# Chunked delta rule and attention layer on one core: which waits the scan's operands have, the order of turns and sums, and when masks are made

## The reference

```
h = rms_norm(x, norm_w);  proj = h @ w_in            # q, k, v, z, beta, decay, sw_q, sw_k, sw_v, sw_z
qkv = silu(conv5(q, k, v));  q, k = l2_norm(q) * 128**-0.5, l2_norm(k)
g = cumsum(-exp(a_log) * softplus(decay + dt_bias))  # per chunk
decay = exp(g[c] - g[s]), s <= c
m = strict_lower((k * beta) @ k.T * decay)
t_inv = inverse(I + m)
u = t_inv @ (v * beta);  w = t_inv @ (k * beta * exp(g))
a = lower(q @ k.T * decay)
for each chunk:                                      # the scan, state S
    v_new = u - w @ S
    o = (q * exp(g)) @ S + a @ v_new
    S = S * exp(g_last) + (k * exp(g_last - g)).T @ v_new
dn = rms_norm(o_forward + o_backward) * silu(z)
sw = window_attention(rope(norm(sw_q)), rope(norm(sw_k)), sw_v) * silu(sw_z)
x = x + concat(dn, sw) @ w_out
```

## Time and profile before

| | |
|---|---|
| median of three runs | 1055.47 us (1055.0 to 1056.21) |
| the profiled execution | 1055.53 us, of which the span is 1053.7 us |
| TensorE busy | 973.8 us |
| DVE, ACT, POOL busy | 497.8, 470.3, 450.2 us |
| mean granted clock of TensorE | 0.977 |

### The profile page before, as it was taken

One profiled execution on the slowest core, in us unless ns is written; L12 is line 12 of the kernel. 1 busy time (PEld: TensorE's weight loads), 2 busy tenths in 40 slices (PEclk: granted clock), 3 DMA queues, 4 the chain that ended last, 5 costly groups with the idle time before them and its releaser, 6 DMA issues.

```text
span 1053.7 us, 12811 instructions
## 1 busy us (share of the span) xinstructions
PE 973.8 (92%) x5186; PEld 821.5 (78%) x5186; DVE 497.8 (47%) x812; ACT 470.3 (45%) x822; POOL 450.2 (43%) x254
## 2 busy tenths in 40 slices
PE   7999797659999899999999979899999999999987
PEld 6987576659999797777777758788888888888876
DVE  4066763597675354424246432433333333564434
ACT  6565566435654244433476441453433433342223
POOL 4537443660002464243577642254353444454440
PEclk9999999869999999999999999999999999999998
DMA  9522200000010017133312221133223232323302
GB/s 343 167 65 88 80 21 1 1 1 1 2 56 27 1 50 243 41 119 100 100 61 61 79 81 61 59 102 102 98 89 111 80 116 85 100 100 100 100 20 81
DMA packets 25306, 84.07 MB, mean 80 GB/s; under 512 B 3008, under 2 KB 3264, under 8 KB 25120
## 3 DMA queue, kind: packets, MB, share of 16 engines
q1 hardware_dynamic: 24240, 81.88, 23.4%
q10 hardware_dynamic: 1008, 1.38, 0.4%
HBM read 79.06 MB, written 2.10 MB: 77 GB/s over the span
## 4 chain that ended last, share of the span: by engine, by line
PE 75%; DVE 12%; ACT 8%; POOL 3%; issue 2%; DMA 0%; DVEq 0%; ACTq 0%
PE bank L1910 73%; DVE qk L1460 2%; PE bank L1918 2%; ACT wh L1127 1%; ACT L1127 1%; DVE xl L1454 1%; DVE dd L1454 1%; DVE vc L1460 1%; DVE mp L1454 1%; ACT ee L1127 1%; ACT xs L1127 1%; POOL wl L1015 1%; DVE xf L1454 1%; ACT qk L1127 1%; ACT xh L1127 1%
## 5 line engine op out<-in xcount | busy, mean ns | idle before, releaser
L1015 POOL TENSOR_TENSOR wl<-raw,wh 128x1024 fp32r<-128x1024 f32 (+1 forms) x130 | 313.6, 2417 | 382.5 <-ACT wh L1127 382.5
L1910 PE MATMUL bank<-xh,wh 128*128 128x512 f32 (+1 forms) x536 | 207.8, 388 | 6.8 <-DVE xl L1454 4.8
L1910 PE MATMUL bank<-xh,wl 128*128 128x512 f32 (+1 forms) x536 | 206.0, 384 | 0.0
L1910 PE MATMUL bank<-xl,wh 128*128 128x512 f32 (+1 forms) x536 | 206.0, 384 | 0.0
L1127 ACT ACTIVATE wh<-raw 128x1024 fp32r<-128x1024 f32 (+2 forms) x132 | 135.8, 1036 | 133.2 <-PE bank L1910 127.4
L1910 PE MATMUL bank<-wh,xh 128*128 128x512 f32 (+1 forms) x352 | 141.2, 401 | 14.8 <-DVE xl L1460 7.0
L1910 PE MATMUL bank<-wh,xl 128*128 128x512 f32 (+1 forms) x352 | 136.0, 386 | 0.0
L1910 PE MATMUL bank<-wl,xh 128*128 128x512 f32 (+1 forms) x352 | 135.9, 386 | 0.0
L1910 PEld LDWEIGHTS bank<-xh,wh 128*128 128x128 f32 x536 | 101.5, 189 | 27.9 <-issue 5.9
L1910 PEld LDWEIGHTS bank<-xh,wl 128*128 128x128 f32 x536 | 101.5, 189 | 19.9
L1910 PEld LDWEIGHTS bank<-xl,wh 128*128 128x128 f32 x536 | 101.5, 189 | 19.1
(11 more groups left out here) (250 smaller groups left out, 1563.7 us busy)
## 6 DMA issues: line engine op xcount, KB each, us to landing
raw<-in_wflat SPq DMA_DIRECT2D x126, 512.0 KB, 3.5
xt<-in_xt SPq DMA_DIRECT2D x8, 256.0 KB, 4.9
h<-in_x SPq DMA_DIRECT2D x4, 512.0 KB, 7.5
h<-in_x SPq DMA_DIRECT2D x1, 2048.0 KB, 8.8
gain<-in_pr SPq DMA_DIRECT2D x3, 512.0 KB, 3.7
consts<-in_cf SPq DMA_DIRECT2D x1, 1472.0 KB, 11.4
raw<-in_wflat SPq DMA_DIRECT2D x4, 272.0 KB, 11.3
kh<-kh SPq DMA_DIRECT2D x8, 128.0 KB, 2.3
```

The source lines that it names most:

```text
L1015: e.tensor_tensor(WL[u % NS][:, 0:n], RAW[u % NS][:, 0:n], WH[u % NS][:, 0:n].bitcast(F32), ALU.subtract).then_inc(w_lo.up(u), 1)
L1910: return e.matmul(o, l, r_, start=start, stop=stop, skip_group_check=part)
```

## The change

- In the scan POOL's first `vb` waits for chunk 0's inverse, no longer for chunk 2's too. `kb` doesn't wait for `av` of the round before; it waits for the last `nw`, which reads the same tile, and only from round 2 on. `vb` waits for `av`.
- The norms take banks 6, 7, 4, 5 in turn, and `g1` moves on by 2, 3, 3 and 4 steps behind the sz units (before 3 each), so that all eight exponentials are in front of the z stage.
- The gate turns of chunk 0 stand behind the first and second z unit, and ahead of the steps of `g1` there.
- `dd` (DVE) and `mr` (ACT) of a chunk are made one step of the inverse later, at the head of the step with the transposes. On ACT the function `inv_mr` (before: `inv_m`) is what the new step `inv_dd` calls.

```diff
@@ -522,6 +522,7 @@
         BI.let_go(("inv", cb, "k"))
         do("inv_m", cb)
         yield
+        do("inv_dd", cb)
         for d in range(2):
             take(("mt", d), (inv_v, ("dt", cb, 0, d)))
         do("inv_mt", cb)
@@ -578,7 +579,7 @@
     G.over((0, 1, 2, 3))
     g1 = in_turn(qk_norm(), to_tokens("v"), rope_turn(), to_tokens("k"))
 
-    def tok_part(u0, n, by, *sides):
+    def tok_part(u0, n, by, norms):
         ids, i = G.ids, G.i
         G.over((0, 1, 2, 3))
         for tb in range(4):
@@ -587,11 +588,11 @@
         for k in range(4):
             w_ahead(u0 + k + 2)
             do("tok", u0, k, "n0", SLOT0, n)
-            for g, m in sides:
-                step(g, m)
-
-    G.over((4, 5, 6, 7))
-    tok_part(U_SZ, 512, lambda tb: (proj, ("sz", tb)), (g3, 1), (g1, 3))
+            step(g3)
+            step(g1, norms[k])
+
+    G.over((6, 7, 4, 5))
+    tok_part(U_SZ, 512, lambda tb: (proj, ("sz", tb)), (2, 3, 3, 4))
     gi = [invert(cb) for cb in (0, 3, 1, 2)]
     BI.over((4,))
     ids, i = G.ids, G.i
@@ -602,9 +603,9 @@
     for k in range(4):
         w_ahead(U_Z + k + 2)
         do("tok", U_Z, k, "n0", SLOT0, 512)
+        if k < 2:
+            step(gi[0])
         step(g1, 4)
-        if k in (1, 2):
-            step(gi[0])
     while step(g1):
         pass
     step(gi[1], 2)
@@ -1076,17 +1077,17 @@
             W = SCAN[d]
             if r == 0:
                 on.wait_ge(*inv_v.at(("t", 0, 1)))
-                on.wait_ge(*inv_v.at(("t", 2, 1)))
                 on.wait_ge(*swa_g.at(3))
-            else:
-                on.wait_ge(*scan_p.at(("av", d, r - 1)))
             on.wait_ge(*gate_v.at("beg"))
             on.wait_ge(*gate_a.at("egl"))
             on.wait_ge(*tok_a.at(("k", cb)))
             on.wait_ge(*tok_a.at(("v", cb)))
             k3 = h3(KT[:, cb, :])
             if r:
+                if r > 1:
+                    on.wait_ge(*scan_p.at(("nw", d, r - 1)))
                 e.tensor_tensor(h3(W["KB_"][:]), k3, b4r(BEG[:, d, cb, :]), ALU.mult).then_inc(scan_g.up(("kb", d, r)), 1)
+                on.wait_ge(*scan_p.at(("av", d, r - 1)))
             e.tensor_tensor(h3(W["VB"][:]), h3(VT[:, cb, :]), b4r(BETA[:, d, cb, :]), ALU.mult).then_inc(scan_g.up(("vb", d, r)), 1)
             if r < 3:
                 e.tensor_tensor(h3(W["KD"][:]), k3, b4r(EGL[:, d, cb, :]), ALU.mult).then_inc(scan_g.up(("kd", d, r)), 1)
@@ -1277,7 +1278,7 @@
             on.wait_ge(*inv_a.at(("ee1", cb, d)))
             act(ee, ee, ACT.Exp, inv_a.up(("ee", cb, d)), scale=-1.0)
 
-        def inv_m(cb):
+        def inv_mr(cb):
             for d in range(2):
                 on.wait_ge(*inv_g.at(("m", cb, d)))
                 act(WORK[cb]["MR"][d][:], MP[cb][:, d, :], ACT.Copy, inv_a.up(("mr", cb, d)))
@@ -1439,7 +1440,7 @@
             e.dma_start(ov[:, tb, 0:512], OUT[:, tb, 0:512]).then_inc(s_out[0], 16)
 
...
                     gm_root=gm_root, up_post=up_post,
@@ -1622,6 +1623,9 @@
             for d in range(2):
                 on.wait_ge(*inv_g.at(("mb", cb, d)))
                 tt(MP[cb][:, d, :], psum[b][:, :], W["MB"][d][:], ALU.mult, inv_v.up(("m0", cb, d)))
+
+        def inv_dd(cb):
+            W = WORK[cb]
             for d in range(2):
                 on.wait_ge(*inv_g.at(("m", cb, d)))
                 tt(h3(W["DD"][d][:]), h3(MP[cb][:, d, :]), bc4(cf("LM", 7 * (1 - d))), ALU.mult, inv_v.up(("dd", cb, 0, d)))
@@ -1895,7 +1899,7 @@
                 stt(OUT[:, tb, c], H[:, tb, c], rr, GAIN[:, c], ALU.mult, ALU.mult, fin_v.up(("out", tb, n)))
 
...
```

More of the change, by code:

```diff
@@ L1441, in scalar_engine @@
         return dict(begin=begin, x_split=x_split, rms_row=rms_row, prep=prep, prep_half=prep_half, stat=stat, split=split, conv=conv, square=square, qsum=qsum, qexp=qexp, to_tok=to_tok,
-                    gate1=gate1, gate2=gate2, rope_root=rope_root, rope_t=rope_t, tok=tok, inv_decay=inv_decay, inv_m=inv_m,
+                    gate1=gate1, gate2=gate2, rope_root=rope_root, rope_t=rope_t, tok=tok, inv_decay=inv_decay, inv_dd=inv_mr,
                     inv_d=inv_d, swa_s=swa_s, swa_t=swa_t, swa_o=swa_o, scan_keys=scan_keys, scan_v=scan_vn, scan_o=scan_o,
@@ L1897, in vector_engine @@
         return dict(begin=begin, x_split=x_split, conv_rms=conv_rms, scale=scale, split=split, masks=masks, conv=conv, qexp=qexp, gate1=gate1, gate2=gate2, rope_sq=rope_sq,
-                    rope_root=rope_root, rope_scale=rope_scale, rope=rope, rope_t=rope_t, inv_decay=inv_decay, inv_kq=inv_kq, inv_m=inv_m,
+                    rope_root=rope_root, rope_scale=rope_scale, rope=rope, rope_t=rope_t, inv_decay=inv_decay, inv_kq=inv_kq, inv_m=inv_m, inv_dd=inv_dd,
                     inv_mt=inv_mt, inv_x=inv_x, inv_d=inv_d, inv_x7=inv_x7, inv_t=inv_t, swa_s=swa_s, swa_t=swa_t, swa_o=swa_o,
```

## The result

The changed kernel takes 1120.34 us (median of 4 runs, 1120.01 to 1121.9), the one before 1055.5 (4 runs). The ratio is 1.0617, interval 1.0604 to 1.063: 6.2% slower, where 1038.8 us, 1.6% faster, was predicted. The profiled execution took 1120.64 us.

What follows compares the result with a forecast made beforehand. TensorE, busy for 92% of the span, was taken as the bound, so only its waits or lower clock could be won. A 7.0, B 2.0, C 0.8, D 2.0 and E 4.9 sum to 16.7 us: 1038.8 us, range 1034 to 1043.

Steps and rivals of the forecast that it cites:

- D: Inverse: with the dd masks one step later, DVE no longer waits for POOL's mp; 2.0 us won.
- Rival 4: z stage: the wait at 149.6 us drops the clock and short waits keep it down; 1061 us, chance 0.02.
- rival 1: z stage: the clock falls at the new 3.0 us wait at 149.6 us; 1040.6 to 1044.7 us, chance 0.11.
- A: Norms: sums in banks 6 and 7 first lose their waits, z starts at 142.7 us; 7.0 us won.
- rival 2: v turn: DVE and POOL products hold the gate longer, so the norms' lead is lost; 1045.3 us, chance 0.08.
- B: z stage: chunk 0's earlier gate turns end the qhl and kll waits, adding one of 3.0 us; 2.0 us won.
- C: Chunk 3's gate turn no longer waits for kt in bank 4; 0.8 us won.
- E: Scan: first vb product 3.0 us earlier, shorter waits for kb worth 1.9 us; 4.9 us won.

Runs made afterwards that it cites:

- e4: The changed kernel with 24 extra 512-column matmuls in front of chunk 0's level 2 of the inverse: 1059.74 us, ratio 1.0039.
- e5: The kernel before with 16 extra DVE products ahead of chunk 0's mask at level 3 of the inverse: 1113.18 us, ratio 1.0544.
- e12: The kernel before with 9 extra DVE products ahead of chunk 0's mask at level 3 of the inverse: 1110.34 us, ratio 1.0502.
- e1: The kernel before with only the dd masks and mr copies moved one step later: 1134.84 us, ratio 1.0744.
- e2: The changed kernel with the dd masks and mr copies back where they were: 1042.28 us, ratio 0.9865.
- e11: e3 plus the norms' new bank order and g1 steps, with gate turns and dd where they were: 1048.48 us, ratio 0.9916.
- e3: The kernel before with only the new waits of vb and kb in the scan: 1047.72 us, ratio 0.9918.
- e7: e2 with chunk 0's gate turns behind the second and third z unit: 1039.42 us, ratio 0.9845.
- e8: The changed kernel with 24 extra 512-column matmuls in front of chunk 1's second transposes: 1121.68 us, ratio 1.0622.
- e9: e8 with chunk 0's gate turns behind the second and third z unit: 1120.25 us, ratio 1.0608.
- e14: e7 with dd and mr two steps later still, behind the xf of level 1 of the inverse: 1121.69 us, ratio 1.0629.

## Why the prediction was wrong

**The step that failed** is D, and with it the reading of the clock. D asked what the move wins DVE (2.0 us; DVE now goes from the first `mp` to the first `xf` of level 1 in 25.3 us, 200.83 to 226.12, against 26.9, 207.01 to 233.87, so 1.6). It did not ask who stands behind the moved `dd`. The order quoted for the change shows `mx` behind them, and TensorE's score product waits for `mx`; the earlier trace rows gave the price, 3.4 us for each pair. Two pairs in front of one `mx` are 6.8 us on top of the two `dt` pairs, so a wait of some 5 us could have been estimated. (D's own sum also has 3.4 where its rows say 3.1; with 3.1 it gives the 2.0 that it took.)

The price of such a wait was then the second mistake. Rival 4 had the mechanism, a lower clock that stays, but put it in the z stage, at 2 in 100. There the clock did fall, at the wait I named, which is rival 1; it came back by 160, with wide matmuls, as after 124 us in the earlier trace rows. The rows of before held the warning at the other place: 0.50 in 215 to 225 us and 0.74 in 225 to 230, so the inverse (from 233.19) began just after the clock had returned. The stops there (4.04 and 4.28) were also longer than the 3.34 that the prediction called the longest gap. I never looked at that stretch's clock, and took the level in the inverse for granted. The runs showed in its place that the inverse has two lasting levels under the same work (e4, e5, e12), and that the move of `dd` decides between them: 78 to 79 us (e1, e2) where D said 2.0 won.

**A** was right: no wait at the sums, z at 142.74 (142.7). It is worth nothing alone (e11), since DVE's queue was the next limit: rival 2's mechanism, at a later turn than it named.

**B** was mis-sized: 6.45 us for the new wait, not 3.0, beyond its upper bound of 6. Two things were missed. DVE's rope products stood ahead of the `qk` products and were long beside POOL's `wl` (3.83 us for three; the next such group took 1.63), so the `qk` began at 147.57; and four `qk` took 7.87 us, 1.97 each in place of 1.56. The first scores came 5.4 us earlier (184.70 for 190.07) instead of 9.8. By times, A, B and C together are 5.4 us (e3 less e2); a later place for the gate turns makes them 8.3 (e3 less e7).

**C** came as forecast: no wait for `kt` is left.

**E** was right at the start (3.05 us for 3.0; one `kb` wait of 0.58 for 0.6), and too small for the rest: 3.4 by the trace for 1.9, so 6.5 for 4.9.

Without D the change is e2's 1042.28 us, where the same sum gives 1040.8 (1038.8 + 2.0). One term decided the sign.

## What to carry to other kernels

When an operation is moved within a queue, price first who stands behind it, above all what the matrix engine waits for; what the queue itself wins comes second. In a long stretch of small products, as this inverse is, look at the clock as a state: read at which level it enters, how near that is to the level's change, and price every new stop ahead of or inside it with the whole stretch at half rate (here some 185 us, some 80 us lost, for a stop of 5). Stops of 6.45 and 4.28 us were forgiven where other work followed: wide matmuls in the z stage, the row of transposes in the kernel before. And an idle stretch on an engine that another one feeds is no gain until the next limit in that feed has been read.

## What the runs showed that I had not expected

A TensorE that is busy for 100 of 100 us does not come back to its higher level by that alone: some 185 us of the inverse's products stayed at 0.50, and the same products stayed at 1.00 to the inverse's end after e4's wide matmuls. Nor does it take wide matmuls. In the kernel before the clock came back behind 128-column transposes, and in all seven kernels whose inverse ran at 0.50 (after, e1, e5, e8, e9, e12, e14) it came back within the inverse's last level, again 128 columns wide. In the kernel's code the transposes and the last level read `mp` as plain float32 (the last level adds bfloat16 products), the levels between read `fp32r` tiles; whether that is the difference no run tests. A stop of 3.79 us was enough to go down (e12), and in e8 waits under 0.8 us; stops of 4.04 and 4.28 us in the kernel before did no lasting harm. DVE's product of 512 columns took 0.68 us undisturbed, 1.74 (`dd`) and 1.97 (`qk`) beside POOL.
